# Differential pairs' second maps scaled and merged on VectorE alone, GpSimd left with the other maps' scaling

## The reference, cut to what matters

```python
def diff_attend(q, kvs, lam, scale):
    s = jnp.concatenate([jnp.einsum('bhmqd,bhmkd->bhmqk', q, k, preferred_element_type=jnp.float32)
                         for k, _ in kvs], axis=-1) * scale
    p = jax.nn.softmax(s, axis=-1)
    w = p[:, :, 0] - lam * p[:, :, 1]
    ...
```

## Time and profile before

| | |
|---|---|
| runs | 2317.91, 2319.37, 2321.66 us; median 2319.37 us |
| profiled execution | 2314.69 us, of which the trace's span is 2312.9 us |
| pair attention, layer 0 | about 156 to 250 us of the span |
| pair attention, layer 1 | about 768 to 833 us of the span |

### The profile page before, as it was taken

How to read it: one execution, slowest core, us unless ns; L and a number is a source line. 1 busy time by engine, 2 the same in 40 slices (tenths; PEclk the granted TensorE clock), 3 DMA queues, 4 the chain that set the end, 5 groups by cost and what they waited for, 6 DMA issues and landing times.

```text
span 2312.9 us, 46122 instructions
## 1 busy us (share of the span) xinstructions
PE 2266.2 (98%) x17107; PEld 2077.8 (90%) x17107; DVE 1558.4 (67%) x2787; ACT 1207.1 (52%) x2090; POOL 149.7 (6%) x246
## 2 busy tenths in 40 slices
PE   8998999999999999999999999999999999999998
PEld 6786888888888789999999989999999999899998
DVE  5656688887877568865656846666466558467764
ACT  5647444443236656654445565644454456656553
POOL 0226200000110410000000000000000000000000
PEclk9999999999999999999999999999999999999999
DMA  9740234444644025555555334455545554354664
GB/s 339 237 165 1 98 112 156 145 138 162 199 139 150 19 85 191 180 181 167 181 171 158 129 98 149 146 184 170 174 153 182 168 161 137 101 167 151 204 192 125
DMA packets 103166, 356.41 MB, mean 154 GB/s; under 512 B 11392, under 2 KB 15136, under 8 KB 103040
## 3 DMA queue, kind: packets, MB, share of 16 engines
q1 hardware_dynamic: 89248, 306.55, 41.2%
q0 software_dynamic: 13792, 48.14, 6.4%
HBM read 352.55 MB, written 1.05 MB: 153 GB/s over the span
## 4 chain that ended last, share of the span: by engine, by line
PE 92%; DVE 3%; ACT 3%; issue 1%; DMA 1%; ACTq 0%; DVEq 0%; POOL 0%; SPq 0%
PE ps L845 26%; PE ps L847 25%; PE ps L846 25%; PE ps L862 1%; PE ps L866 1%; PE ps L1020 1%; PE ps L863 1%; PE ps L1055 1%; PE ps L1039 1%; PE ps L933 1%; PE ps L1390 1%; PE ps L972 1%; PE ps L1348 1%; PE ps L1319 1%; ACT probs L1571 1%
## 5 line engine op out<-in xcount | busy, mean ns | idle before, releaser
L2052 DVE TENSOR_TENSOR wl<-raw,wh 128x1024 fp32r<-128x1024 f32 x571 | 698.2, 1223 | 394.8 <-ACT wh L1482 394.4
L845 PE MATMUL ps<-hH,wh 128*128 128x272 f32 (+2 forms) x2880 | 884.7, 307 | 4.1 <-DVE silu L2823 3.1
L846 PE MATMUL ps<-hL,wh 128*128 128x272 f32 (+2 forms) x2880 | 873.3, 303 | 0.0
L847 PE MATMUL ps<-hH,wl 128*128 128x272 f32 (+2 forms) x2880 | 873.1, 303 | 0.0
L1482 ACT ACTIVATE wh<-raw 128x1024 fp32r<-128x1024 f32 x571 | 599.6, 1053 | 303.8 <-PE ps L847 287.8
L845 PEld LDWEIGHTS ps<-hH,wh 128*128 128x128 f32 x2880 | 543.5, 189 | 32.9 <-issue 4.1
L846 PEld LDWEIGHTS ps<-hL,wh 128*128 128x128 f32 x2880 | 543.7, 189 | 20.0 <-issue 0.2
L847 PEld LDWEIGHTS ps<-hH,wl 128*128 128x128 f32 x2880 | 543.5, 189 | 19.9
L847 PE MATMUL ps<-actH,wl 128*128 128x272 f32 (+2 forms) x1184 | 358.4, 303 | 0.0
L845 PE MATMUL ps<-actH,wh 128*128 128x272 f32 (+2 forms) x1184 | 356.3, 301 | 0.2 <-ACT actH L1693 0.2
L846 PE MATMUL ps<-actL,wh 128*128 128x272 f32 (+2 forms) x1184 | 356.3, 301 | 0.0
(11 more groups left out here) (344 smaller groups left out, 2854.6 us busy)
## 6 DMA issues: line engine op xcount, KB each, us to landing
raw<-in_w_ffn_gu SPq DMA_DIRECT2D x176, 512.0 KB, 3.5
raw<-in_w_mix SPq DMA_DIRECT2D x98, 512.0 KB, 3.5
raw<-in_w_up SPq DMA_DIRECT2D x88, 512.0 KB, 3.5
raw<-in_w_ffn_down SPq DMA_DIRECT2D x64, 512.0 KB, 3.5
ada_rest<-in_w_ada POOLq DMA_DIRECT2D x32, 512.0 KB, 4.8
raw<-in_w_out SPq DMA_DIRECT2D x32, 512.0 KB, 3.7
raw<-in_w_down SPq DMA_DIRECT2D x32, 512.0 KB, 3.5
weights_a<-in_w_ada POOLq DMA_DIRECT2D x24, 512.0 KB, 3.7
```

What stands on the lines that cost most here:

```text
L845: pe.matmul(out, a_h, b_h, start=start, stop=False)
L846: pe.matmul(out, a_h, b_l, start=False, stop=False)
L847: return pe.matmul(out, a_l, b_h, start=False, stop=stop)
L2052: dve.tensor_tensor(wl[:, slot, :], raw[:, slot, :], wh[:, slot, :].bitcast(F32), ALU.subtract).then_inc(l_split, 1)
```

## The change

VectorE's `merge` treats both halves of the map, with `hinv` for both halves multiplied by minus lambda in the one small instruction. GpSimd skips m = 1 steps; its scaling has one multiplication in place of two (the second was by lambda or by 1.0). `pair_scaled` therefore counts only the steps that are not m = 1. TensorE's turn waits for `pair_merged` alone in a differential pair and for `pair_scaled` alone in another. ScalarE's wait for a slot of an m = 0 step is for `pair_merged` alone. The semaphore `second_scaled` goes.

```diff
                 for st in pair_steps(l):
+                    if st.m:
+                        continue
                     pool.wait_ge(pair_inv, st.g + 1)
                     for i, (c, u) in enumerate(st.maps()):
-                        if st.m and c == 0:
-                            continue
                         w = probs[:, st.g % 4, c, u * st.nk:(u + 1) * st.nk]
-                        last = pool.tensor_scalar(w, w, hinv[:, st.g % 4, i:i + 1], lam[:, l, 6:7] if st.m else 1.0, ALU.mult,
-                                                  ALU.mult)
-                    if st.m:
-                        last.then_inc(second_scaled, 1)
-                        pool.wait_ge(second_scaled, st.d + 1)
-                        w = probs[:, st.g % 4, 1, 0:st.cols]
-                        last = pool.tensor_tensor(w, w, probs[:, (st.g - 1) % 4, 1, 0:st.cols], ALU.add)
+                        last = pool.tensor_scalar(w, w, hinv[:, st.g % 4, i:i + 1], None, ALU.mult)
                     last.then_inc(pair_scaled, 1)
...
                 def turn(st):
-                    pe.wait_ge(pair_scaled, st.g + 1)
                     if st.diff:
                         pe.wait_ge(pair_merged, st.d + 1)
+                    else:
+                        pe.wait_ge(pair_scaled, st.g - st.d + 1)
...
                     before = run[st.n - 4]
-                    act.wait_ge(pair_pt, before.t + 1) if before.turns else act.wait_ge(pair_scaled, before.g + 2)
-                    if not before.turns:
+                    if before.turns:
+                        act.wait_ge(pair_pt, before.t + 1)
+                    else:
                         act.wait_ge(pair_merged, before.d + 1)
...
                 dve.wait_ge(pair_inv, st.g + 1)
-                scale = hinv[:, st.g % 4, 0:st.tiles]
+                scale = hinv[:, st.g % 4, 0:2 * st.tiles]
                 link(dve.tensor_scalar(scale, scale, lam[:, l, 6:7], None, ALU.mult))
-                dve.wait_ge(pair_scaled, st.g)
-                for u in range(st.tiles):
+                dve.wait_ge(pair_scaled, st.g - st.d)
+                for i, (c, u) in enumerate(st.maps()):
                     keys = slice(u * st.nk, (u + 1) * st.nk)
-                    w = probs[:, st.g % 4, 0, keys]
-                    last = dve.scalar_tensor_tensor(w, w, hinv[:, st.g % 4, u:u + 1], probs[:, (st.g - 1) % 4, 0, keys], ALU.mult,
+                    w = probs[:, st.g % 4, c, keys]
+                    last = dve.scalar_tensor_tensor(w, w, hinv[:, st.g % 4, i:i + 1], probs[:, (st.g - 1) % 4, c, keys], ALU.mult,
                                                     ALU.add)
                 last.then_inc(pair_merged, 1)
```

More of the change, by code:

```diff
@@ L412, in build_program @@
         pair_scaled = sem("pair_scaled")
-        second_scaled = sem("second_scaled")
         pair_merged = sem("pair_merged")
```

## The result

The changed kernel takes 2340.64 us (median of 4 runs, 2335.40 to 2342.56) against 2320.14 for the kernel before, run beside it. The ratio is 1.0083, 95% interval 1.0069 to 1.0097, which is 16 to 22 us slower. The forecast was +2.3 us with a range up to 2326. It was wrong. Medians are of all executions; four executions on record lay far above the rest (2764.58, 3156.78, 4452.66 and 6538.90 us), and the ratios and intervals leave them out.

What follows compares the result with a forecast made beforehand. TensorE was taken as the bound. Longer VectorE merges add 1.82 us in layer 0 and 0.60 in layer 1, less 0.11 regained, all else 0: +2.3 on 2319.37 gives 2321.7 us, range 2317.5 to 2326.

Steps and rivals of the forecast that it cites:

- What bounds the kernel: TensorE, busy 98%; its largest attention wait is for VectorE's copy behind the merge, 2.8 us in each layer.
- What is added to VectorE: Merges in both attentions: +0.30 us per single tile, +0.61 per two tiles; +2.3 us in all reaching TensorE.
- The slow rival: VectorE's merge instruction itself costs its 1.12 us, not a wait for GpSimd: +7.3 us, 2326.7; chance 0.08.
- What is taken from GpSimd: Ten merges' second-map scaling (0.76 us) and addition (1.58) removed: 0 on the path, with 1.05 us of slack before the turn.
- The fast rival: TensorE's turns waited for GpSimd's addition, so VectorE's earlier finish is won: 6.6 us faster, 2312.8; chance 0.04.
- The one-multiplication scaling on GpSimd: Form shown nowhere; taken as 0.68 us, or 0.76; cost 0, with 1.27 us of room before the n = 4 merge.
- The prediction's signs of error: Merge instruction at 1.1 us or at 0.6 or less, GpSimd wait at the turn gone, or time moving outside the attentions.

Runs made afterwards that it cites:

- the late merge: Kernel before, with VectorE's merge of step i - 2 put behind the maximum of step i, ahead of the reciprocal of step i - 1: 2316.89 us against 2320.43.
- the other late order: Kernel before, with VectorE's merge of step i - 2 put behind the reciprocal of step i - 1: 2322.35 us, ratio 1.0009.
- the one with two multiplications: Changed kernel, but GpSimd's scaling keeps its second multiplication (by 1.0): 2323.46 us against 2319.94 for the kernel before, ratio 1.0013.
- the run with the slow form in the tail: Changed kernel, with one multiplication on GpSimd only behind each layer's last merge, two elsewhere: 2329.20 us against 2320.43 for the kernel before.
- the late merge with both halves: Changed kernel's merge and two multiplications on GpSimd, merge of step i - 2 behind the maximum of step i: 2324.99 us, ratio 1.0015 to the kernel before.

## Why the prediction was wrong, step by step

**What bounds the kernel:** right. TensorE, and the copy behind the merge as its largest wait in the attentions, though with the copy alone moved ahead another wait takes the place of this one.

**What is added to VectorE:** right in every term. The new instructions were to take 0.67 and 0.40 of the engine, so 1.34 for two and 1.60 for four; they take 1.33 and 1.59. The step that charged +2.3 us measured +2.4 in the trace and 3.0 (0.9 to 5.1) in the runs. That the old 1.12 was mostly a wait for GpSimd is borne out too: the same instruction takes 0.75 in the late merge, with no scaling of GpSimd beside it, and 1.18 in the other late order, with one. The slow rival, which took the 1.12 for the instruction's own price, has fallen: no merge instruction of the changed kernel or of the one with two multiplications reaches 0.76.

**What is taken from GpSimd:** the removal was worth 0, as said, since with two multiplications the trace adds up to the merges' cost and nothing else. The fast rival has fallen as well.

**The one-multiplication scaling on GpSimd:** this is the step that failed. The prediction said that no row showed it, took 0.68 from "the nearest rows", which have two operations, and wrote "so with 1.27 of room either value costs 0". It bounded the unknown form by two rows of the other form, and both ends lay on the same side. The instruction takes 1.56 us. Two of them per step are 0.88 x 2 = 1.76 us more, and the room was 1.27. The scalings of n = 2 take 1.76 more as well, against 1.16 of idle time ahead of those of n = 3, so these also start 0.6 late, which makes 0.6 + 1.76 - 1.27 = 1.1 at the merge of n = 4. There, with the scalings of the two steps in a row, the merge starts 176.69 - 173.94 = 2.75 behind the start of VectorE's last maximum, against 173.36 - 171.78 = 1.58 before, so 1.17 later. The rows did offer a wider bound from above, GpSimd's addition at 1.58, another of its instructions at that size. With that as the upper price the room of 1.27 would not have covered two scalings, and the sum would have needed a term for GpSimd at the merges.

**Where a stall goes:** not foreseen at all. A wait of 2 to 3 us on TensorE can cost more than itself, because the clock may fall to half behind it. In the changed kernel steps 7 and 8 lose 1.55 + 1.44 = 3.0 us between the merge of n = 4 and that of n = 7, in rounds where TensorE is busy throughout (180 to 186 us in the windows above), and the clock's whole share is about 6 of the 19 us. The sum had no term for it.

**The slower rival** had the right sign and the wrong engine. The prediction's signs of error had nothing of this either: they name a wait on GpSimd at the turn that is gone, and what the trace shows is one that is new, 2.6 us in layer 0 and 1.7 in layer 1.

## What to carry to other kernels

An edit that looks like a simplification of an instruction is a new instruction: if no row of the trace shows its form, its price is unknown, and it is measured by itself before the rest is argued. On GpSimd `tensor_scalar` with a neutral second operation (times 1.0) beat the one with a single operation by more than two to one at 512 columns. And an instruction's length in a trace may be mostly a wait for another engine, so the same work can be cheaper in another place in the order, as the late merge showed.

## What the runs showed that was not expected

GpSimd's `tensor_scalar` with one operation takes 2.5 ns per column and with two about 0.8, with each of the operands tried (shortest records of one execution); at 512 columns 1.56 against 0.68 us. No run shows why.

The granted clock of TensorE fell to 0.50 in the attention behind idle stretches of 1.99, 3.05 and 1.92 us in the changed kernel, of 1.61 in the run with the slow form in the tail and of 1.16 in the late merge with both halves, and stayed there for some 3 to 7 us. In the late merge it fell once more, behind two short stretches, 0.97 and 0.46 us. In the first case it fell as TensorE started again, behind the other four of the five stretches named first 0.7 to 1.9 us later. It did not fall behind every such stretch: 1.61 us of waiting at n = 7 cost nothing in the run with two multiplications, and in the changed kernel the clock stayed at 1.00 behind this one:

```profile
200.29 1.08 PE L1049 MATMUL ps<-probsT,v_tok 128*64 128x256 f32 x8 [2.29 <-DVE probsT L2271]
...
200.00:204.00 4.00, 3.21 (x23) 2.13 (x24) 2.65 (x5) 2.69 (x7) 2.56 (x2) 1.00 0.00 0
```

So the length of the wait alone does not decide it, and what does stays open. The Trainium skill (TensorE: Matmul & The Clock Gate, Part 1: The HAM clock gate) says that the clock is at half when the engine has been idle and that activity releases it. The traces agree in so far as every fall stands behind idle time and the clock came back to 1.00 while TensorE was busy.
